# First block of the first feed-forward stage: K tile by K tile for both row groups

## The reference, cut to what matters

```python
def rmsnorm(x, g):
    xf = x.astype(jnp.float32)
    y = xf * lax.rsqrt(jnp.mean(xf * xf, axis=-1, keepdims=True) + EPS)
    return (y * g.astype(jnp.float32)).astype(x.dtype)

def swiglu(x, w_gate, w_up, w_down):
    return (jax.nn.silu(x @ w_gate) * (x @ w_up)) @ w_down

x = x + 0.5 * swiglu(rmsnorm(x, ff1_norm[l]), ff1_w_gate[l], ff1_w_up[l], ff1_w_down[l])
```

## Time and profile before

| | us |
|---|---|
| median of 3 runs | 1212.55 (1212.38 to 1216.47) |
| the profiled execution | 1213.13 |
| its span | 1211.1 |
| busy in it: TensorE | 1200.7 |
| VectorE | 937.1 |
| ScalarE | 675.9 |

### The profile page before, as it was taken

The page is one execution under the profiler, slowest core; times in us unless marked ns, Lnnn a source line. Parts: engine busy times, 40 slices in busy tenths (PEclk is TensorE's granted clock), DMA queues, the critical chain, the costliest instruction groups (busy, mean ns, idle before and its releaser), DMA issues.

```text
span 1211.1 us, 16264 instructions
## 1 busy us (share of the span) xinstructions
PE 1200.7 (99%) x6100; PEld 1011.2 (83%) x6100; DVE 937.1 (77%) x1386; ACT 675.9 (56%) x970; POOL 41.9 (3%) x85
## 2 busy tenths in 40 slices
PE   9999999999999999999999999999999999999997
PEld 7888888888778888888888888888888888888886
DVE  5999997756676666888987677786887777687797
ACT  6566655446666455665646554565554454566561
POOL 2000002100000000000000001000000000000000
PEclk9999999999999999999999999999999999999999
DMA  7676566754545556666557656566566544756552
GB/s 265 204 201 197 177 209 199 250 173 149 149 146 174 176 190 202 181 193 190 187 181 180 204 182 222 173 192 201 182 215 209 164 139 139 237 183 192 189 188 73
DMA packets 150909, 225.83 MB, mean 186 GB/s; under 512 B 8152, under 2 KB 85984, under 8 KB 150832
## 3 DMA queue, kind: packets, MB, share of 16 engines
q1 hardware_dynamic: 148304, 216.10, 56.2%
q0 software_dynamic: 2512, 8.69, 2.7%
q10 hardware_dynamic: 16, 0.00, 0.0%
HBM read 223.72 MB, written 1.05 MB: 186 GB/s over the span
## 4 chain that ended last, share of the span: by engine, by line
PE 97%; DVE 2%; DMA 0%; ACT 0%; issue 0%; SPq 0%; DVEq 0%
PE ps L691 23%; PE ps L603 17%; PE ps L610 16%; PE ps L618 16%; PE ps L695 12%; PE ps L528 3%; PE ps L671 2%; PE ps L668 2%; PE ps L673 2%; DVE wl L1767 1%; PE ps L858 1%; PE ps L871 1%; DMA raw<-in_ff_w_gate_dram 0%; PE ps L1074 0%; PE ps L841 0%; PE ps L1044 0%
## 5 line engine op out<-in xcount | busy, mean ns | idle before, releaser
L1767 DVE TENSOR_TENSOR wl<-raw,wh 128x1024 fp32r<-128x1024 f32 (+1 forms) x405 | 476.9, 1197 | 79.8 <-ACT wh L1145 78.0
L1145 ACT ACTIVATE wh<-raw 128x1024 fp32r<-128x1024 f32 (+1 forms) x405 | 409.0, 1034 | 61.6 <-PE ps L618 14.3
L691 PE MATMUL ps<-XT,wh 128*128 128x512 f32 x1216 | 423.0, 392 | 0.0
L695 PE MATMUL ps<-XT,wl 128*128 128x256 f32 x1216 | 339.7, 279 | 0.0
L691 PEld LDWEIGHTS ps<-XT,wh 128*128 128x128 f32 x1216 | 227.6, 187 | 50.9
L695 PEld LDWEIGHTS ps<-XT,wl 128*128 128x128 f32 x1216 | 229.5, 189 | 0.2
L603 PE MATMUL ps<-wh,XT 128*128 128x512 f32 x510 | 203.4, 399 | 0.3 <-ACT wh L1696 0.3
L610 PE MATMUL ps<-wl,XT 128*128 128x512 f32 x510 | 199.4, 391 | 0.5 <-DVE wl L2606 0.5
L618 PE MATMUL ps<-wh,XT 128*128 128x512 f32 x510 | 158.0, 391 | 0.0
L603 PEld LDWEIGHTS ps<-wh,XT 128*128 128x128 f32 x510 | 95.8, 188 | 21.6 <-ACT wh L1696 1.1
L610 PEld LDWEIGHTS ps<-wl,XT 128*128 128x128 f32 x510 | 95.9, 188 | 20.5 <-DVE wl L2606 1.7
(11 more groups left out here) (339 smaller groups left out, 1393.3 us busy)
## 6 DMA issues: line engine op xcount, KB each, us to landing
raw<-in_ffn_w_gu_dram SPq DMA_DIRECT2D x88, 512.0 KB, 4.3
raw<-in_w_in_dram SPq DMA_DIRECT2D x56, 512.0 KB, 3.8
raw<-in_ff_w_up_dram SPq DMA_DIRECT2D x44, 512.0 KB, 4.6
raw<-in_ff_w_down_dram SPq DMA_DIRECT2D x44, 512.0 KB, 3.9
raw<-in_ffn_w_down_dram SPq DMA_DIRECT2D x44, 512.0 KB, 4.2
raw<-in_ff_w_gate_dram SPq DMA_DIRECT2D x40, 512.0 KB, 4.5
raw<-in_gla_w_in_dram SPq DMA_DIRECT2D x24, 512.0 KB, 4.5
raw<-in_moba_w_in_dram SPq DMA_DIRECT2D x24, 512.0 KB, 4.5
```

The source lines that it names most:

```text
L691: e.matmul(o, wh_of(j)[:, w], XT[:, kt, :, :].rearrange("p a n -> p (a n)"), start=kt == 0, stop=False)
L695: ins = e.matmul(o[:, 0:256], wl_of(j)[:, w], XTH[:, kt, :], start=False, stop=kt == kts - 1)
L1145: e.activation(wh_of(j)[:, 0:m], source(j), ACT.Copy).then_inc(S("wh"), 1)
L1767: e.tensor_tensor(wl_of(j)[:, 0:m], source(j), wh_of(j)[:, 0:m].bitcast(F32), ALU.subtract).then_inc(S("wl"), 1)
```

## The change

Row group 1 takes each K tile of the first block directly behind row group 0. x10 is loaded ahead of chunk 1, and x01 and x11 ahead of chunk 2. TensorE has a routine of its own for the block (`pe_start`), ScalarE and VectorE split x and weights in the matching order, and on both the iterator of `f1g0` is called with a tail of 0 for network 1.

```diff
-        plan_aux_x(1, ROWS)
+        plan_aux_x(1, [(0, 0), (1, 0), (0, 1), (1, 1)])
...
+            load_x(0, 0)
+            load_half(0, 0)
+            load_half(0, 1)
+            load_x(1, 0)
+            load_half(1, 0)
+            load_half(1, 1)
+            for t in range(2):
+                load_x(t, 1)
+            for j in range(2, HALVES):
...
+        def pe_start(e, name):
+
+            wait = wait_x(1)
+
+            def three(t, kt):
+                j, c = divmod(kt, 2)
+                w, o = cols(c), ps[:, bank_of(name, t), :]
+                if t == 0:
+                    e.wait_ge(S("wh" if c else "wh_first"), j + 1)
+                wait(e, "h", t, kt)
+                e.matmul(o, XTH[:, kt, rows(t)], wh_of(j)[:, w], start=kt == 0, stop=False)
+                if t == 0:
+                    e.wait_ge(S("wl" if c else "wl_first"), j + 1)
+                e.matmul(o, XTH[:, kt, rows(t)], wl_of(j)[:, w], start=False, stop=False)
+                wait(e, "l", t, kt)
+                return e.matmul(o, XTL[:, kt, rows(t)], wh_of(j)[:, w], start=False, stop=False)
+
+            three(0, 0)
+            e.wait_ge(S("x10"), 16)
+            e.wait_ge(S("x_low"), 1)
+            pe_turn_pieces(e, 1)
+            three(0, 1)
+            three(1, 0)
+            three(1, 1).then_inc(S("used"), 1)
+            three(0, 2)
+            pe_turn_x(e, 1, 0, 1)
+            three(1, 2)
+            pe_turn_x(e, 1, 1, 1)
+            three(0, 3)
+            three(1, 3).then_inc(S("used"), 1)
+            for j in range(2, HALVES):
+                for t in range(2):
+                    pe_products(e, name, t, j, XTH, XTL, wait)
+
+        def pe_turn_pieces(e, t):
+            key = ("x", 1, t, 0)
+            pe_wait_free(e, key)
+            for k in range(4):
+                if t == 1 and k < 2:
+                    e.wait_ge(S("x_low"), k + 1)
+                ins = e.transpose(turned_piece(key, k), X[:, t, rows(k)], ident[:, :])
+            pe_last_fill(key, ins)
...
-                for t in block(f"{f}g0", 4):
+                for t in block(f"{f}g0", 0 if f == "f1" else 4):
...
+            high_x(key, 0).then_inc(S("x_high"), 1)
+            high_half(0, 0)
+            high_x(key, 1).then_inc(S("x_high"), 1)
+            high_x(key, 2)
+            high_x(key, 3).then_inc(high(key)[0], 1)
+            high_half(0, 1)
+            key = ("x", 1, 1, 0)
+            e.wait_ge(*filled(key))
             for k in range(2):
                 high_x(key, k).then_inc(S("x_high"), 1)
-                high_half(0, k)
             high_x(key, 2)
             high_x(key, 3).then_inc(high(key)[0], 1)
             for h in range(2):
                 high_half(1, h)
...
+            for t in range(2):
+                split_x(1, t, 1)
                 for h in range(2):
-                    high_half(j, h)
...
+                    high_half(2 + t, h)
```

More of the change, by code:

```diff
@@ L456, in turned_piece @@
         def turned_piece(key, k):
-            if key == ("x", 1, 0, 0) and k < 2:
+            if key in (("x", 1, 0, 0), ("x", 1, 1, 0)) and k < 2:
                 return ps[:, 7 - k, P:2 * P]
@@ L491, in load_half, with load_x @@
                 e.dma_start(raw[:, j, cols(h)], src[:, h, :]).then_inc(S(f"raw{j}" if h else f"raw{j}first"), 16)
[L493 to L499, removed]
+            def load_x(t, h):
+                e.dma_start(X[:, t, cols(h)], x[0, rows(t), cols(h)]).then_inc(S(f"x{t}{h}"), 16)
+            load_x(0, 0)
[7 more added lines that the diff above has]
+            for j in range(2, HALVES):
                 for h in range(2):
                     load_half(j, h)
-            e.dma_start(X[:, 1, cols(1)], x[0, P:2 * P, cols(1)]).then_inc(S("x11"), 16)
             for j in loads[HALVES:]:
@@ L553, in wait_x, with wait_start @@
             whole = wait_parts(lambda t, half: ("x", stage, t, half))
-            def wait_first(e, part, t, kt):
-                if t == 0 and kt < 2:
-                    e.wait_ge(S("x_high" if part == "h" else "x_low"), kt + 1)
-                else:
-                    whole(e, part, t, 0 if t == 0 and kt == 2 else kt)
-            return wait_first if stage == 1 else whole
+            def wait_start(e, part, t, kt):
+                if kt < 2:
+                    e.wait_ge(S("x_high" if part == "h" else "x_low"), 2 * t + kt + 1)
+                else:
+                    whole(e, part, t, 0 if kt == 2 else kt)
+            return wait_start if stage == 1 else whole
         def idle(e, n):
@@ L583, in pe_products @@
+        def pe_turn_pieces(e, t):
[6 more added lines that the diff above has]
+            pe_last_fill(key, ins)
         def pe_products(e, name, t, j, lh, ll, wait, between=(0, ())):
-            if t == 0 and j == 0:
-                pe_first_products(e, name, wait)
-                return
@@ L603, in pe_products @@
                 e.matmul(o, lh[:, kt, rows(t)], high[:, w], start=kt == 0, stop=False)
-                if t == 0 and j == 2 and c == 0:
-                    pe_turn_x(e, 1, 1, 0)
                 if t == 0 and j < HALVES:
@@ L649, in pe_seven @@
                 e.wait_ge(*emptied(("rsb", f)))
-                e.wait_ge(*((S("x_low"), 2) if f == "f1" else (S("yl"), 8)))
+                e.wait_ge(*((S("x_low"), 4) if f == "f1" else (S("yl"), 8)))
             elif first and f == "f3":
@@ L751, in wait_h @@
                     e.wait_ge(S("hh" if part == "h" else "hl"), len(NARROW) * FFNS.index(f) + kt // 2 - 1)
-            pe_first(e, f"{f}g0", stage, halves)
+            if f == "f1":
+                pe_start(e, "f1g0")
+            else:
+                pe_first(e, f"{f}g0", stage, halves)
             for now in pe_gemm(e, f"{f}u0", XTH, XTL):
@@ L1111, in pe_program @@
             e.transpose(ps[:, 2, 0:8], SC[0:8, 0, 0:P], ident[0:8, 0:8]).then_inc(S("gturn"), 1)
-            key = ("x", 1, 0, 0)
             e.wait_ge(S("x00"), 16)
[L1114 to L1117, removed]
+            pe_turn_pieces(e, 0)
             idle(e, 3)
-            pe_ffn(e, "f1", 1, [(1, 1)])
+            pe_ffn(e, "f1", 1, ())
             pe_mixer(e)
@@ L1280, in ffn @@
                         if f == "f1":
-                            e.wait_ge(S("x_low"), 2)
+                            e.wait_ge(S("x_low"), 4)
                             for r in range(2):
@@ L1707, in act_program @@
                 high_half(1, h)
-            split_x(1, 0, 1)
-            for j in range(2, HALVES):
+            for t in range(2):
+                split_x(1, t, 1)
                 for h in range(2):
-                    high_half(j, h)
-            for h in range(2):
-                split_x(1, 1, h)
+                    high_half(2 + t, h)
             at_chunk["next"] = HALVES
@@ L2607, in low_half @@
                     S("wl" if h else "wl_first"), 1)
[L2610 to L2620, removed]
+            first, second = ("x", 1, 0, 0), ("x", 1, 1, 0)
+            low_half(0, 0)
+            for k in range(2):
+                e.wait_ge(S("x_high"), k + 1)
+                low_piece(first, k).then_inc(S("x_low"), 1)
+            low_half(0, 1)
+            for k in range(2):
+                e.wait_ge(S("x_high"), k + 3)
+                low_piece(second, k).then_inc(S("x_low"), 1)
+            e.wait_ge(*high(first))
+            low_piece(first, 2)
+            low_piece(first, 3).then_inc(emptied(first)[0], 1)
+            low_half(1, 0)
+            e.wait_ge(*high(second))
+            low_piece(second, 2)
+            low_piece(second, 3).then_inc(emptied(second)[0], 1)
+            low_half(1, 1)
+            for t in range(2):
+                low_x(1, t, 1)
                 for h in range(2):
-                    low_half(j, h)
+                    low_half(2 + t, h)
             at_chunk["next"] = HALVES
-            ffn("f1", 1, [(1, 0), (1, 1)], [rotary()])
+            ffn("f1", 1, [], [rotary()])
             mixer()
```

## The result

The changed kernel takes 1216.80 us (median of 7 runs, 1216.31 to 1218.6) against 1212.38 for the kernel before (median of 7 runs beside it, 1212.12 to 1216.47): a ratio of 1.0038, 95% interval 1.0029 to 1.0048. That is 4.4 us more, where 1216.3 was forecast. The profiled execution took 1216.46, its span is 1214.3.

The account below looks back on a forecast made before the run. TensorE's opening plus an unbroken matmul stream bounds the kernel. VectorE's wait for the positions loses 3.7 us, the first block's 1.3 gain inside it: 1216.8 for the profiled execution, 1216.3 against the median, range 1214.4 to 1218.6.

Parts of the forecast that it names:

- What bounds it: Whole run: opening plus an unbroken matmul stream on TensorE, so a microsecond won or lost in the opening reaches the end.
- The first block: f1g0 on TensorE: better fed by the new order, it ends at 19.9 instead of 21.18, a gain of 1.3 us.
- (a) The squares: ScalarE, f1g0: chunks 4 to 7 go ahead of the squares, which begin at 21.0, 3.6 us later.
- the forecast's lower bound: ScalarE's squares begin at 19.75 if chunk 7's load never holds it; the loss is then 2.5 us in all.
- (b) The count of the steps: VectorE, f1g0: four Nones put the wait for pos ahead of chunk 8; pos lands at 28.45, a 6 us stand.
- The chain behind the cast: VectorE's queue to the f1u0 readouts: 9.6 us from the cast, readouts from 38.0, next long matmul 39.85; loss 3.7.
- the second wait: TensorE at the f1u0 (HBf) turns: a wait ended by VectorE's readout, after the 3.4 us stand for diag.
- rival A: TensorE behind the diag stand: clock falls to half, 2.7 us less work done, 1.6 adds at the turns; 1217.8; chance 0.14.
- The sum: Whole run: span 1211.1 plus 2.0 outside plus 3.7 is 1216.8; against the median, 0.6 lower, 1216.3.
- B: f1g0: VectorE is not held for pos; 0.2 gained, 1212.3, or with early squares 1.3, 1211.3; chance 0.10.
- C: First block: not fed better, ends at 21.2; time stays 1216.3, or 1217.6 with squares later by 1.3; chance 0.10.

Follow-up runs that it names:

- e1: Changed kernel with the f1g0 iterator back at a tail of 4 on ScalarE and VectorE, new order kept; 1213.54 us.
- e9: Kernel before, in its old order, with the f1g0 iterator's tail at 0 and the rotary side work three steps later; 1212.24 us.
- e10: Repeat of e2 on the chip of e9: changed kernel with the rotary side work three steps later; 1211.91 us.
- e4: Kernel before, in its old order, with the f1g0 iterator's tail at 0 and VectorE's two x11 splits placed ahead of it; 1215.80 us.
- e8: Kernel before with one unused 128x512 sum on VectorE ahead of the f1u0 readouts; 1214.63 us.
- e3: Changed kernel with GpSimd's load of the positions issued ahead of rms(1) instead of behind it; 1214.66 us.
- e6: Changed kernel with twelve unused 128x128 matmuls on TensorE ahead of its wait for diag; 1216.55 us.
- e11: Changed kernel unaltered, run again on the chip of e9 and e10; 1216.71 us.
- e7: Changed kernel with VectorE's four small operations for diag moved from behind chunk 8 to ahead of the wait for the positions; 1217.72 us.
- e2: Changed kernel with the side work three empty steps later (VectorE 3 to 6, ScalarE 11 to 14), tail still 0; 1211.85 us.
- e5: Changed kernel with the tail of 4 back and the side work one empty step later (VectorE 4, ScalarE 12); 1213.78 us.

## Why the prediction held, step by step

**What bounds it: right, with a limit.** A loss of 3.2 at M was a loss of 3.2 in the span. But the stream behind M has two paces (last section): in e1's profiled execution 0.8 won at M didn't reach the end.

**The first block: right in its end, too large in its gain.** Forecast 19.9, measured 19.68. The gain was put at 1.3 against the earlier trace rows's 21.18; e9 against e10 makes it 0.5. The term of the sum that was off is the base. In the old order `f1u0` begins at 20.30, 20.46 and 20.37 in e4, e8 and e9, on three chips, and only in the profile of before at 21.18 (in the new order at 19.68 to 20.15 in eight executions, at 20.63 in e3). The late piece stands in the very chain that the prediction read: the second weight chunk. ScalarE's two halves of it in before and in e9:

```profile
8.40 1.24 ACT L1696 ACTIVATE wh<-raw 128x512 fp32r<-128x512 f32 x2 [1.22 <-DMA raw<-in_ff_w_gate_dram]
```

```profile
7.56 1.29 ACT L1696 ACTIVATE wh<-raw 128x512 fp32r<-128x512 f32 x2
```

They began at 7.62 in e8 and 7.37 in e4. So some 0.8 of the 1.3 was one late landing in one execution, and not what the new order can win.

**(a) The squares: mis-sized, 19.28 for 21.0.** Chunk 7's load, issued at 14.8, took 3.5 and not the 4.9 of the earlier trace rows, so it never held ScalarE. That was the forecast's lower bound, 19.75; the other 0.5 is that ScalarE left the first block at 15.33 and not at 15.9.

**(b) The count of the steps: right,** cast ahead of chunk 8. From the first square to the issue of the load 4.71 (forecast 4.75). To landing 3.8 instead of 2.7, a term that was mis-sized. With the squares 1.7 early, and the landing 1.1 late, the cast came at 27.77 and not 28.45: two errors that partly cancel. The stand of VectorE was 6.25 (forecast 6). The longer landing goes with the change and isn't chance alone. The stretch from issue to landing, before and then after (the last two numbers are the busy share of the DMA engines and GB/s):

```profile
22.15:24.85 2.70, 2.70 (x14) 2.23 (x13) 2.59 (x3) 2.70 (x4) 1.52 (x2) 1.00 0.23 50
```

```profile
23.99:27.79 3.80, 3.80 (x18) 3.00 (x16) 0.02 (x1) 3.80 (x5) 1.52 (x2) 1.00 0.94 321
```

With chunks 4 to 7 split early the raw buffers come free early. From 14 to 22 us SyncE issues six weight loads in after and two in before, and the small load lands among them.

**The chain behind the cast: right.** 9.56 from cast to readouts (forecast 9.6), M 2.0 behind them (forecast 1.85). M at 39.33 instead of 39.85 is the cast's 0.7 carried on, less small change. D at 30.88 for 31.55 likewise. Wrong in it is the second wait, foreseen at the turns: the halved clock, which the forecast left to rival A, filled it (e6 brings it back, 0.99).

**The sum.** 3.2 in the profiled executions where 3.7 was said, and 4.4 in the medians. With e9's opening M of before would be 0.8 earlier, at 35.34, and the loss in the traces 39.33 - 35.34 = 4.0. The prediction took its 3.7 from the M of an execution that lay 0.6 above the median, and added it to the median. With the earlier base the same working gives 39.85 - 35.34 = 4.5, some 1217.1. So 1216.3 was as near to 1216.80 as it was because the chain was put 0.5 too long and the base 0.8 too late, and these work against each other; that is luck. Of the 0.4 between 4.0 and 4.4 some 0.2 is the mix of runs: three of seven of after are at 1217.48 or more, one of seven of before is at 1216.47, and without these the medians are 4.2 apart. The rest isn't assigned; M differs by 0.3 between two executions of this very kernel (39.33, and 39.62 in e11).

**The rivals.** A: its clock fall came, its price didn't. Behind the stand of 2.87 the granted clock was 0.57. The Trainium skill, TensorE: Matmul & The Clock Gate, Part 1, "The HAM clock gate", has an idle array go back to half rate; in this the trace agrees. A had 2.7 us of TensorE's work lost and 1.6 of it at the turns. Measured are 1.6 lost (7.65 from D to the turns for 6.01) and some 0.15 at M (e6, e4 against after, e11): the rest was covered by the wait for the readouts. With that cover taken away (e7) it costs more: M comes 0.47 later though the readouts begin at the same time. B: refuted, VectorE was held; its thought that the late squares alone would cost little holds only with the side steps behind the readouts (e2), not otherwise (e3). C: wrong that the block isn't fed better, as it ended at 19.68 and not at 21.2; right in its doubt, as the order's own gain is 0.5 and not 1.3.

## What to carry to other kernels

Changing how an iterator yields moves all side work that hangs on its yields: count the yields, and look for the step that waits for something made downstream of the same stage. The price of such a wait is the queue behind it on its engine, up to the last result another engine needs: take one consumer out of the queue (e7) and the same time is lost at the next. A load that is moved may land later because other loads moved with it. And one profile of the kernel before is a base with an error of its own, here 0.8 us, more than half of the gain put down to the new order; that its execution lay 0.6 above the median was a warning.

## What the runs showed of the hardware

**Two paces of the same matmuls.** The stages of narrow blocks (288 pairs of 128x512 and 128x256, four such stages in a run) go at 346.8 or at 353.3 ns a pair, and mostly keep it for the whole stage: 1.9 us each. Groups of TensorE from 50 to 130 us, before and then e1 (busy us, mean ns of one):

```profile
L691 PE MATMUL ps<-XT,wh 128*128 128x512 f32 x232 | 80.5, 391 | 0.0
```

```profile
L718 PE MATMUL ps<-XT,wh 128*128 128x512 f32 x227 | 80.3, 399 | 0.0
```

In the same 80 us e1 does 5 pairs fewer, at a granted clock of 1.00. In e1 this turned a lead of 1.1 into a lag of 1.0 by 147 us, a second slow stage late in the run brought it to 3.0, and run times gather at steps of about 1.9 (1212.2, 1214.1, 1216). What chooses the pace is open. In the first such stage the slower one sets in directly behind the turns in e1, e3, e7 and e8. All four had a wait in those turns, but so had e4 and e6, which went fast; the seven kernels without one began fast. In the fourth stage e1 and e5 were slow behind turns of the usual length. So such a wait is neither enough nor needed; whether it makes the slower pace likelier is open. e5 turned slow in the middle of its first stage, where TensorE's weight load stood 0.36 us for VectorE (its timelines of PEld and of PE):

```profile
65.91 0.19 PEld L718 LDWEIGHTS ps<-XT,wh 128*128 128x128 f32 x1 [0.36 <-DVE SGf L1923]
```

```profile
65.91 0.50 PE L718 MATMUL ps<-XT,wh 128*128 128x512 f32 x1
```

The share differs by chip (5 of 27, 12 of 24 and 2 of 21 runs of before were high). That e2 and e10 had none in 21 runs may be chance.

**The opening** differs between executions of one order. D is at 28.54, 28.62 and 29.35 in the old order, and what moved it was the landing of the second weight chunk (8.4 in before). It wasn't the pace of the first long matmul, which lasts 0.79 in all three.

**The clock** fell behind stands of 2.87, 2.72 and 3.91 us (0.57, 0.65, and 0.72 in e7), not behind one of 1.73 (e4). In after and e11 it read 1.00 again from 36 us on. It read 1.00 in e6, where TensorE worked through most of the stand.

**A 1 KB load by GpSimd**, the positions, took 2.7 us to land where the DMA engines were busy 0.21 to 0.72 of the time (before, e1, e5, e8, e9), 3.1 at 0.80 (e4), 3.5 to 3.8 at 0.90 to 1.05 (after, e2, e6, e7, e10, e11), and 6.1 in the opening (e3, 0.97).
